# A diffusion layer with product-key experts: 28 multiply-adds handed to ScalarE and GpSimd, 13 steps moved ahead, gate chunks on GpSimd's queue

## The chip, the cores and the metric

The kernel runs on one core of one Trainium2 chip. The metric is device time in microseconds (us) of one execution. The core has TensorE (PE in the profile), VectorE (DVE), ScalarE (ACT), GpSimd (POOL), and SyncE (SP), which here only issues transfers.

## The reference, cut to what matters

One layer is computed for 128 context tokens (tile 0) and 512 latent tokens (tiles 1 to 4). Its second half is a retrieval over 16384 single-neuron experts:

```
def _peer(h, w_query, sub_keys, expert_u, expert_v):          # per block of 128 tokens
    q = (xb @ w_query).reshape(t, 8, 2, 128)
    s = einsum('thik,hink->thin', q, sub_keys)                # 8 heads, two halves of 128 keys
    v_half, i_half = top_k(s, 16)
    top_v, top_pos = top_k(v_half[0] + v_half[1] (16 x 16), 16)
    idx = i_half[0] * 128 + i_half[1] at top_pos              # 8 x 16 = 128 picks per token
    g = softmax(top_v)
    act = gelu(einsum('thkd,td->thk', expert_u[idx], xb))
    return einsum('thk,thkd->td', g * act, expert_v[idx])
```

Each token has 128 picks. For each pick the kernel needs a dot product with a row of `expert_u` (1024 numbers) and a multiply-add of a row of `expert_v`.

## The kernel before, in words

The program of each engine is written out by hand, in order, with semaphores between the engines. Up to about 1340 us of the profiled execution it does the token-mixing half of the layer; the change does not touch that. The retrieval is done in two ways.

**Gathered tiles.** Context tile 0 and latent tiles 1 and 2 (the code calls the latter "apart") have their rows gathered: for pick k GpSimd issues an indirect DMA of 128 rows of 4 KB (512 KB) of `peer_u` (`u_row`) and one of `peer_v` (`v_row`). VectorE does the dot (`u_dot`, line 1999) and the multiply-add into a sum of 128 x 1024 (`v_add`, line 2021; semaphore `vc_used` counts them). The v side runs 20 picks behind the u side for the context (`LEAD`) and 40 behind for the apart tiles (`APART_LEAD`). A "context step" j is `u_dot(j)` and `v_add(j - 20)`, 148 of them; an "apart step" j is `u_dot(128 + j)` and `v_add(128 + j - 40)`, 296 of them. The rows land in ten buffers of 4 KB a partition; the u rows and the v rows use four each, for some stretches eight, and GpSimd waits in `row_free` until the row that stood in the buffer has been used. GpSimd's loop interleaves the u row of step j and the v row of step j in one queue.

**Whole tiles.** Tiles 3 and 4 are done densely. PE multiplies them with blocks of all of `peer_u` (128 blocks of 512 KB, `s_block`, line 1112; ScalarE takes each with a Gelu, line 1531, `take_s`), the result is multiplied with a gate matrix, and PE multiplies that with the blocks of `peer_v` (`v_block`, line 1143). The gate matrix is built from one-hot rows in 64 units (the "build": VectorE lines 2168 and 2178, ScalarE lines 1566 and 1557, PE line 1130). Half of the gates stays in SBUF, half goes to HBM (`gates_far`), comes back in 16 chunks of 512 KB made of 512-byte pieces (`load_gates`, two buffers, on SyncE's queue between the expert blocks) and is multiplied in by GpSimd (`gate_block`, line 1702, 64 of them).

**The order of the last half.** Stretches, by what VectorE and PE do:

1. Heads (from 1410 us). PE makes queries in 16 halves (line 1070) and scores, ScalarE copies them out (`take_queries`, lines 1484 to 1493). VectorE finds for each head the 16 best of tiles 3 and 4 (two calls of `top`), then runs `CTX_BESIDE[h]` context steps, for some heads a `top` of an apart tile, and `APART_BESIDE[h]` apart steps; at head 6 it finishes tile 0 (`result(0, ...)`), which needs ScalarE's `tile_norm(0)`.
2. First half of the blocks. PE runs 64 `s_block`s. ScalarE's program pins other work to them by number n: `tile_norm(0)` behind n = 20, the Exp of the whole tiles' weights (`ew_done`, line 1542) behind n = 44, and the Exp and Gelu of the first apart items (`gates`, lines 1329 and 1330) behind n = 54, 58 and 62. VectorE meanwhile does `SOFTMAX_AT` = 8 apart steps, `weigh_whole` (line 2157, needs `ew_done`), and the rest of `APART_EARLY` steps. From apart step 40 on a v row is added, and ahead of it `weights(8)` (line 2009) needs the `gates` behind n = 54. `APART_TOP_AT` says behind which step a `top` of an apart tile stands.
3. Build, with single apart steps between the units (`APART_BUILD`).
4. Between: 64 pairs of `v_block` and `s_block` on PE, and 104 apart steps spread beside them (`START_BETWEEN`). `gate_block(n)` stands in GpSimd's queue behind step `START_BETWEEN + (20 + n) * 104 // 64`.
5. Last: 64 `v_block`s of the second half, all remaining apart steps, the last results.

```
CTX_BESIDE = (5, 5, 5, 5, 4, 4, 0, 0)
APART_TOP_AT = {16 * n - 9: n for n in range(3, 2 * PH)}
APART_EARLY = 34
APART_BUILD = [int(u % 6 == 1) for u in range(UNITS)]
START_1 = sum(APART_BESIDE) + APART_EARLY
```

Of the kernel before, what the change touches and what calls it, by code (L numbers as in the profile page):

```python
# [5 lines left out]

# [65 lines left out]
def q_end(who, name):  # L72
    return Q[who, name] + len(TILES[who])
# [78 lines left out]
def row_slot(kind, k):  # L152

    j = k - PICKS
    if kind == "u":
        if j < 0:
# [4 lines left out]


ROW_ORDER = ([row for j in range(PICKS + LEAD) for row in [("u", j)] * (j < PICKS) + [("v", j - LEAD)] * (j >= LEAD)]
             + [row for j in range(2 * PICKS + APART_LEAD)
# [132 lines left out]
def layer_kernel(nc, a, outs):  # L297

    y_out, st_out = outs
    with ExitStack() as ctx:  # L300
# [130 lines left out]
        rowbuf = [at(kb, D) for kb in (166, 170, 174, 186, 92, 96, 190, 194, 110, 114)]  # L431
        pv_c, pv_a = at(135.25, D), [at(16, D), at(178, D)]
        tables_c = [at(125.75 + 0.5 * i, PICKS) for i in range(3)]
        tables_a = [at(kb, 2 * PICKS) for kb in (198, 199, 108)]
# [36 lines left out]
        def s(name):  # L471
            if name not in S:
# [9 lines left out]
                 "keys_in keys_l_in fq_full fq_out fs_full fs_out sc_full sc_free topk_done topw_done ge_done w_done u_used "  # L482
                 "vc_used pv_done out_ready out_done ew_done gw_done tw_full tw_out ieq_done ihot_done jhot_done "
                 "g_full g_done gs_staged gm_done s_full s_out av_done dve act waited")
# [28 lines left out]
        def _(sp):  # L513
# [142 lines left out]

            far = gates_far.rearrange("g p (i t) -> p g i t", i=HALF)

            def load_gates(c):

                if c >= 2:
                    sp.wait_ge(s("gm_done"), CHUNK * (c - 1))
                sp.dma_start(gates_in[c % 2], far[:, :, CHUNK * c:CHUNK * c + CHUNK, :]).then_inc(gates_sem[c % 2], 16)

            for n in range(HALF):
# [4 lines left out]
            for q in range(2):  # L670
                sp.wait_ge(staged_out[q], 8 * GROUPS)
            chunks = iter(range(HALF // CHUNK))
            for n in range(HALF, len(BLOCKS)):
                load_block(n)
                passed = (n - HALF) // 2 if n < 3 * HALF else HALF + (n - 3 * HALF) // 2
                if n == HALF + NSLOT:
                    load_gates(next(chunks))
                    load_gates(next(chunks))
                if n % 2 and passed >= MULT_LAG + 7 and (passed - MULT_LAG - 7) % CHUNK == 0:
                    c = next(chunks, None)  # L680
                    if c is not None:
                        load_gates(c)
            for c in chunks:
                load_gates(c)
            sp.wait_ge(s("out_done"), 16 * NT)
# [480 lines left out]
        def _(act):  # L1166
# [339 lines left out]

            late = list(range(GATES_DONE, PH))
            take_queries(0, (0,))
            take_queries(1, (0,))
# [10 lines left out]
            take_scores(PH - 1)  # L1520

            def take_s(n, i):
# [10 lines left out]
            for n, i in enumerate(FIRST_ORDER):  # L1533
                take_s(n, i)
                if n == 20:
                    act.wait_ge(s("vc_used"), PICKS)
# [44 lines left out]
            for n, item in enumerate(APART_GATES.get(("last",), [])):  # L1581
                gates(item)
                if n == 0:
                    act.wait_ge(s("vc_used"), 2 * PICKS)
# [17 lines left out]
            store(4, 4)  # L1602
            act.wait_ge(s("vc_used"), 3 * PICKS)
            ch.n += 2
# [6 lines left out]
        def _(pool):  # L1611
# [33 lines left out]
            def row_free(kind, k):  # L1645

                before = ROW_BEFORE[ROW_NUMBER[kind, k]]
                if before is not None:
                    kind_before, k_before = ROW_ORDER[before]
                    pool.wait_ge(s("u_used" if kind_before == "u" else "vc_used"), k_before + 1)  # L1650

# [8 lines left out]
            def v_row(k):  # L1660
# [5 lines left out]
                    bass.IndirectOffsetOnAxis(ap=entries(IDX, k), axis=0)).then_inc(row_in[slot], 16)  # L1666

            pool.wait_ge(s("sc_free"), 4)
            for j in range(CSTEPS):
                if j < PICKS:  # L1670
# [24 lines left out]

            rows_of_apart(START_1)
            def gate_block(n):

# [6 lines left out]
            for j in range(START_BETWEEN, ASTEPS):  # L1705
                rows_of_apart(1)
                for n in MULTS_AT.get(j, []):
                    gate_block(n)


        @block.vector
        def _(dve):
# [299 lines left out]
            def v_add(k):  # L2012
# [6 lines left out]
                else:  # L2019
                    dve.wait_ge(s("vc_used"), k)  # L2020
# [140 lines left out]
            def equal(u):  # L2161
# [30 lines left out]
            for h in range(PH):  # L2192
# [84 lines left out]
```

## Time and profile before

| | |
|---|---|
| time, median of 3 runs | 2803.74 us (2794.14 to 2809.4) |
| the profiled execution | 2781.54 us, its span 2779.7 us |
| PE busy | 2354.6 us, 85% of the span |
| DVE busy | 1839.6 us, 66% |
| POOL busy | 1117.4 us, 40% |
| ACT busy | 612.3 us, 22% |
| indirect gathers | 768 of 512 KB, 402.70 MB of 701.59 MB in all |

A row of a timeline gives start, duration, engine, line and operation, output and input, the number of instructions, and in brackets how long the engine sat idle before it and whom it waited for. "DMA share" is the mean busy share of the 16 DMA engines (values a little over 1 are full), GB/s is what they moved. Busy shares over the whole span say little here, since each stretch has its own bound.

### The profile page before, as it was taken

The page shows a single profiled execution, that of the slowest core. Times are in us where ns is not written, and L with a number is a line of the kernel's source. Part 1 is how long each engine was busy: PE and PEld are TensorE (multiplying, and loading weights), DVE is VectorE, ACT ScalarE, POOL GpSimd, SP SyncE. Part 2 cuts the span into 40 slices and gives each one's busy share as a digit, 9 for nine tenths or more (in the row PEclk, how much of TensorE's full clock was granted, in tenths as well). Part 3 has the DMA queues.
Part 4 walks back from the last instruction along what each step waited for, and adds up shares of the span by engine and source line. Part 5 has one row for each costly group of instructions (what it writes and reads, how often), then busy time and mean ns, then how long its engine had stood idle before and what let it go on. Part 6 is the DMA issues. An engine that isn't in the chain of part 4 may idle for free.

```text
span 2779.7 us, 26765 instructions
## 1 busy us (share of the span) xinstructions
PE 2354.6 (85%) x8858; PEld 1476.9 (53%) x8858; DVE 1839.6 (66%) x3451; ACT 612.3 (22%) x1483; POOL 1117.4 (40%) x928
## 2 busy tenths in 40 slices
PE   6998888899999998999979999576899999999500
PEld 1354544544555544578468888465566666444200
DVE  0335767744100569787779997999775677676988
ACT  0113452522211113311222112384000000100010
POOL 0002312221000125777433234525574767666575
PEclk9899999999999999999989999788999999999855
DMA  7601111213284558999765689746998999999998
GB/s 268 222 31 33 51 38 30 68 38 127 74 269 173 177 190 300 380 369 401 270 266 198 234 310 340 295 167 252 406 397 330 390 400 403 386 401 410 373 334 292
DMA packets 251301, 701.59 MB, mean 252 GB/s; under 512 B 20912, under 2 KB 62000, under 8 KB 249904
## 3 DMA queue, kind: packets, MB, share of 16 engines
q0 software_dynamic: 110592, 402.70, 38.6%
q1 hardware_dynamic: 139872, 294.79, 29.4%
q10 hardware_dynamic: 720, 2.62, 0.2%
q8 instruction: 63, 1.03, 0.1%
q14 instruction: 54, 0.44, 0.0%
HBM read 686.93 MB, written 13.11 MB: 252 GB/s over the span
## 4 chain that ended last, share of the span: by engine, by line
PE 53%; DVE 16%; DMA 14%; POOL 8%; issue 5%; ACT 3%; DVEq 0%; SPq 0%; ACTq 0%; POOLq 0%
PE bank L1112 14%; PE bank L896 11%; PE bank L1143 8%; POOL arena L1664 4%; DMA arena<-in_peer_v,arena 4%; PE bank L1070 4%; PE bank L750 4%; DMA arena<-in_peer_v 3%; POOL arena L1656 3%; DVE arena L2168 3%; DVE arena L2021 2%; PE bank L791 2%; DVE arena L1807 2%; DMA arena<-in_w_ada 2%; PE bank L709 2%
## 5 line engine op out<-in xcount | busy, mean ns | idle before, releaser
L1656 POOL DMA_INDIRECT arena<-in_peer_u,arena x384 | 477.1, 1242 | 789.1 <-DVE arena L1999 429.4
L2021 DVE SCALAR_TENSOR_TENSOR arena<-arena 128x1024 f32<-128x1024 f32 x381 | 495.0, 1299 | 118.7 <-DMA arena<-in_peer_v,arena 112.6
L1999 DVE CUSTOM_DVE_ANT_0 arena<-arena 128x1024 f32<-128x1024 f32 x384 | 475.6, 1244 | 147.5 <-DMA arena<-in_peer_u,arena 147.1
L1664 POOL DMA_INDIRECT arena<-in_peer_v,arena x384 | 461.4, 1202 | 226.5 <-DVE arena L2021 115.9
L896 PE MATMUL bank<-arena 128*128 128x512 f32 (+1 forms) x1472 | 510.0, 508 | 16.5 <-DMA arena<-in_w_in 6.5
L1143 PE MATMUL bank<-arena 128*128 128x512 f32 x1024 | 453.2, 595 | 22.4 <-DMA arena<-in_peer_v 22.4
L1112 PE MATMUL bank<-arena 128*128 128x256 f32 x2048 | 455.1, 380 | 14.6 <-DMA arena<-in_peer_ut 13.9
L1112 PEld LDWEIGHTS bank<-arena 128*128 128x128 f32 x2048 | 390.4, 191 | 95.8 <-issue 30.1
L896 PEld LDWEIGHTS bank<-arena 128*128 128x128 f32 x1472 | 283.2, 194 | 239.1 <-issue 198.6
L1143 PEld LDWEIGHTS bank<-arena 128*128 128x128 f32 x1024 | 194.4, 191 | 243.3 <-issue 224.0
L750 PE MATMUL bank<-arena 128*128 128x512 f32 x384 | 182.0, 621 | 7.9 <-ACT arena L1207 6.5
L1531 ACT ACTIVATE arena<-bank 128x256 f32<-128x256 f32 x128 | 49.0, 383 | 606.3 <-PE bank L1112 606.2
L1629 POOL TENSOR_TENSOR arena<-arena 128x512 f32<-128x512 f32 x40 | 45.1, 1127 | 268.6 <-ACT arena L1255 268.6
L1620 POOL TENSOR_TENSOR arena<-arena 128x512 f32<-128x512 f32 x32 | 42.5, 1362 | 257.2 <-DVE arena L1818 257.2
L1130 PE MATMUL bank<-arena 128*128 128x128 f32 x512 | 86.1, 335 | 62.7 <-ACT arena L1566 62.6
L750 PEld LDWEIGHTS bank<-arena 128*128 128x128 f32 x384 | 72.9, 198 | 87.1 <-issue 83.3
L1130 PEld LDWEIGHTS bank<-arena 128*128 128x128 f32 x512 | 78.8, 242 | 70.2 <-ACT arena L1566 41.2
L1070 PE MATMUL bank<-arena 128*128 128x256 f32 x512 | 112.9, 381 | 0.7 <-ACT arena L1458 0.7
L709 PE MATMUL bank<-arena,cond_sb 128*2 128x512 f32 x192 | 84.8, 600 | 27.2 <-DMA arena<-in_w_ada 27.2
L1807 DVE SCALAR_TENSOR_TENSOR arena<-arena,convw_sb 128x644 f32<-128x644 f32 x96 | 99.5, 1037 | 11.4 <-DVE arena L1807 1.1
L1070 PEld LDWEIGHTS bank<-arena 128*128 128x128 f32 x512 | 97.3, 191 | 13.9 <-ACT arena L1458 1.0
L1255 ACT ACTIVATE arena<-bank,arena 128x128 f32<-128x128 f32 x320 | 86.6, 396 | 50.9 <-PE bank L841 50.7
(237 smaller groups left out, 2389.4 us busy)
## 6 DMA issues: line engine op xcount, KB each, us to landing
arena<-in_peer_ut SPq DMA_DIRECT2D x128, 512.0 KB, 6.9
arena<-in_peer_v SPq DMA_DIRECT2D x128, 512.0 KB, 8.5
arena<-in_w_in SPq DMA_DIRECT2D x22, 2048.0 KB, 9.0
arena<-in_w_ada SPq DMA_DIRECT2D x12, 2048.0 KB, 8.0
arena<-in_w_ssd_out SPq DMA_DIRECT2D x8, 2048.0 KB, 16.2
arena<-in_w_query SPq DMA_DIRECT2D x8, 2048.0 KB, 9.0
arena<-in_w_fourier SPq DMA_DIRECT2D x4, 2048.0 KB, 7.8
arena<-in_w_out SPq DMA_DIRECT2D x4, 2048.0 KB, 13.4
```

The source lines that it names most:

```text
L709: last = mm(bank[slot][0:2, :], cond[:, k, :], w[:, k, :], start=(k == 0), stop=(k == KT - 1))
L750: mm(bank[2][:, :], w[:, k, c0:c0 + P], hT[:, k, P:TOK], start=(k == 0), stop=(k == KT - 1), skip_group_check=True)
L896: last = mm(bank[q % 5][:, 0:cols], rows_of(k), w[:, k, :], start=(k == 0), stop=(k == k_tiles - 1))
L1070: last = mm(bank[n % 4][:, 0:2 * P], w[:, k, c0:c0 + P], h2Tp[1 - pair][:, k, :], start=(k == 0), stop=(k == KT - 1))
L1112: last = mm(bank[4 + n % 2][:, 0:2 * P], ut[:, k, :], h2Tp[1][:, k, :], start=(k == 0), stop=(k == KT - 1))
L1130: last = mm(bank[GATE_BANKS[u % 6]][:, P * t:P * t + P], hot_j[u % HOTS][:, t, :], hot_i[u % HOTS][:, t, :], start=True, stop=True)
L1143: last = mm(bank[2 * t + half][:, :], Aw[:, i % HALF, t * P:t * P + P], v[:, 512 * half:512 * half + 512], start=(i == 0), stop=(i == NKEY ...
L1656: nc.gpsimd.indirect_dma_start(rowbuf[slot], None, a["peer_u"], bass.IndirectOffsetOnAxis(ap=entries(IDX, k), axis=0)).then_inc(row_in[slo ...
L1664: nc.gpsimd.indirect_dma_start(rowbuf[slot], None, a["peer_v"], bass.IndirectOffsetOnAxis(ap=entries(IDX, k), axis=0)).then_inc(row_in[slo ...
L1807: last = STT(o, cin[:, i % 2, k:k + 644], w(k), o, ALU.mult, ALU.add)
L1999: V.tensor_tensor_reduce(out=rowbuf[slot], in0=rowbuf[slot], in1=h2c if item < PH else h2a[:, item // PH - 1, :], scale=1.0, scalar=0.0, o ...
L2021: STT(pv, rowbuf[slot], w, pv, ALU.mult, ALU.add).then_inc(s("vc_used"), 1)
```

## The change

The last 28 picks of the context (k = 100 to 127, `BY_POOL`) are no longer multiplied and added by VectorE. ScalarE scales the gathered row in place with its weight (`scale_rows`), two rows behind each of the halves 2 to 15 of the queries; GpSimd adds the scaled rows into a sum `pv_g` of its own (`add_scaled`, 27 adds of 128 x 1024), and VectorE adds that sum to its own once, at head 5. The `u_dot`s stay on VectorE. A buffer of those v rows comes free by GpSimd's add (`vg_used`), so the gather of row k now waits for the adds of row k - 4 and stands behind `u_row` in the same queue.

The context steps beside the heads become (8, 8, 8, 8, 0, 0, 0, 0), most of them empty. The apart steps ahead of the build go from 24 + 34 = 58 to 24 + 43 = 67, those in the build from 11 to 15; 104 stay between, and 110 are left for the last stretch in place of 123. The `top`s stand 5 steps earlier (steps 34, 50, 66, ...), so three of them and not two are ahead of the build. The second half's gate chunks are issued by GpSimd: two at step 12 of the between stretch, each further one right behind the `gate_block` that frees its buffer. The first one-hot rows wait for block 60 and not 64, and ScalarE's last context gates stand behind half 5 and not 8.

```diff
-CTX_BESIDE = (5, 5, 5, 5, 4, 4, 0, 0)
+CTX_BESIDE = (8, 8, 8, 8, 0, 0, 0, 0)
+BY_POOL = range(100, PICKS)
-APART_TOP_AT = {16 * n - 9: n for n in range(3, 2 * PH)}
-APART_EARLY = 34
+APART_TOP_AT = {16 * n - 14: n for n in range(3, 2 * PH)}
+APART_EARLY = 43
-APART_BUILD = [int(u % 6 == 1) for u in range(UNITS)]
+APART_BUILD = [int(u % 4 == 2 and u < 60) for u in range(UNITS)]
...
@@ sync
             for n in range(HALF, len(BLOCKS)):
                 load_block(n)
-                passed = (n - HALF) // 2 if n < 3 * HALF else HALF + (n - 3 * HALF) // 2
-                if n == HALF + NSLOT:
-                    load_gates(next(chunks))
-                    load_gates(next(chunks))
-                if n % 2 and passed >= MULT_LAG + 7 and (passed - MULT_LAG - 7) % CHUNK == 0:
...
@@ scalar
+            def scale_rows(n, item):
+                for k in itertools.islice(to_scale, n):
+                    slot = row_slot("v", k)
+                    act.wait_ge(s("w_done"), k // TOPK + 1)
+                    act.wait_ge(row_in[slot], 16 * ROW_TURN[ROW_NUMBER["v", k]])
+                    A(rowbuf[slot], rowbuf[slot], ACT.Copy, scale=entries(WTAB, k)).then_inc(s("scaled"), 1)
...
                 if half % 2 == 0:
                     take_scores(half // 2 - 1)
-                if half == 8:
+                if half == 5:
                     for item in late:
                         gates(item)
+                scale_rows(2, 6 if half < 8 else 7)
...
@@ gpsimd
+            def add_scaled(k):
+                pool.wait_ge(s("scaled"), k - BY_POOL[0] + 1)
+                if k == BY_POOL[0]:
+                    return
+                scaled = rowbuf[row_slot("v", k)]
+                if k == BY_POOL[1]:
+                    TT(pv_g, rowbuf[row_slot("v", k - 1)], scaled, ALU.add).then_inc(s("vg_used"), 1)
+                else:
+                    pool.wait_ge(s("vg_used"), v_count(k))
+                    TT(pv_g, pv_g, scaled, ALU.add).then_inc(s("vg_used"), 1)
...
+                if j - LEAD == BY_POOL[4]:
+                    add_scaled(next(to_add))
+                    add_scaled(next(to_add))
+                elif j - LEAD > BY_POOL[5]:
+                    add_scaled(next(to_add))
                 if j >= LEAD:
                     v_row(j - LEAD)
+            for k in to_add:
+                add_scaled(k)
...
+                if j == START_BETWEEN + 12:
+                    for q in range(2):
+                        pool.wait_ge(staged_out[q], 8 * GROUPS)
+                    load_gates(0)
+                    load_gates(1)
                 for n in MULTS_AT.get(j, []):
                     gate_block(n)
+                    if n % CHUNK == CHUNK - 1 and n // CHUNK + 2 < HALF // CHUNK:
+                        load_gates(n // CHUNK + 2)
...
@@ vector
-                if j >= LEAD:
+                if j >= LEAD and j - LEAD not in BY_POOL:
                     v_add(j - LEAD)
...
-                        dve.wait_ge(s("s_full"), HALF)
+                        dve.wait_ge(s("s_full"), max(n + 1 for n in range(HALF) if B_SLOT[n] >= 4))
...
+                if h == 5:
+                    dve.wait_ge(s("vc_used"), BY_POOL[0])
+                    dve.wait_ge(s("vg_used"), len(BY_POOL) - 1)
+                    TT(pv_c, pv_c, pv_g, ALU.add).then_inc(s("vc_used"), 1)
```

## Rows read from the trace of the kernel before

**Rows 1.** Windows: us; PE, PEld, DVE, ACT, POOL busy (instructions); PEclk; DMA share; GB/s.
```profile
1420.00:1540.00 120.00, 119.23 (x613) 106.54 (x614) 99.75 (x317) 24.40 (x59) 30.44 (x24) 1.00 0.51 173
...
1787.00:1912.00 125.00, 86.09 (x512) 78.81 (x512) 125.00 (x227) 99.56 (x320) 33.30 (x24) 0.82 0.46 157
...
2383.00:2500.00 117.00, 111.42 (x258) 48.23 (x256) 81.72 (x121) 10.46 (x16) 78.93 (x68) 1.00 1.03 400
2500.00:2780.00 280.00, 110.13 (x256) 48.56 (x256) 229.83 (x339) 17.18 (x35) 179.41 (x156) 0.71 0.93 352
```

**Rows 2.** Timeline of PE, the end of the first 64 blocks.
```profile
1719.26 41.60 PE L1112 MATMUL bank<-arena 128*128 128x256 f32 x192
```

**Rows 3.** Timeline of DVE, heads to build.
```profile
1439.61 0.43 DVE L1951 MAX8 arena<-arena 128x8 f32<-128x256 f32 x1
...
1448.64 0.43 DVE L1951 MAX8 arena<-arena 128x8 f32<-128x256 f32 x1
...
1453.71 1.22 DVE L1999 CUSTOM_DVE_ANT_0 arena<-arena 128x1024 f32<-128x1024 f32 x1
...
1456.06 1.22 DVE L1999 CUSTOM_DVE_ANT_0 arena<-arena 128x1024 f32<-128x1024 f32 x1
...
1636.60 0.15 DVE L2138 RECIPROCAL arena<-arena 128x1 f32<-128x1 f32 x1
...
1701.91 0.41 DVE L2157 TENSOR_REDUCE arena<-arena 128x16 f32<-128x256 f32 x1
...
1733.37 0.17 DVE L2009 RECIPROCAL arena<-arena 128x1 f32<-128x1 f32 x1 [2.22 <-ACT arena L1330]
...
1787.25 4.96 DVE L2168 TENSOR_TENSOR arena<-shape_consts,arena 128x512 f32<-128x512 f32 x8
```

**Rows 4.** Timeline of ACT in the same stretch.
```profile
1451.52 0.66 ACT L1493 ACTIVATE arena<-bank 128x256 f32<-128x256 f32 x2 [0.30 <-PE bank L1082]
...
1538.21 0.66 ACT L1493 ACTIVATE arena<-bank 128x256 f32<-128x256 f32 x2 [0.30 <-PE bank L1082]
...
1614.48 0.29 ACT L1499 ACTIVATE arena<-arena,eps 128x1 f32<-128x1 f32 x1
...
1696.33 0.42 ACT L1542 ACTIVATE arena<-arena 128x256 f32<-128x256 f32 x1
...
1733.13 0.22 ACT L1330 ACTIVATE arena<-arena 128x16 f32<-128x16 f32 x1
```

**Rows 5.** Timeline of POOL: the gather of u row 124, context.
```profile
1455.21 1.74 POOL L1656 DMA_INDIRECT arena<-in_peer_u,arena  x1 [30.37 <-DVE arena L1999]
```

**Rows 6.** Single lines: count, ns minimum/median/maximum, first and last start, form.
```profile
L1702 POOL TENSOR_TENSOR arena<-arena x64: 723/745/1794, 2031.4 to 2514.0; 128x256 f32<-128x256 f32 x64
...
L1629 POOL TENSOR_TENSOR arena<-arena x40: 1038/1039/1462, 260.1 to 655.8; 128x512 f32<-128x512 f32 x40
...
L1498 ACT ACTIVATE arena<-arena x3: 1040/1048/1056, 1612.0 to 2772.4; 128x1024 f32<-128x1024 f32 x3
```

**Rows 7.** Waits: who waited for whom, us, times, longest.
```profile
POOL arena L1702 <- DMA arena<-gates_far: 80.6, 11, 24.0
```

**Rows 8.** DMA issues: engine, count, KB each, median us to landing.
```profile
arena<-gates_far SPq DMA_DIRECT2D x16, 512.0 KB, 17.7
arena<-in_peer_u,arena POOLq DMA_INDIRECT x384, 8.5
```

**Rows 9.** Windows of line 2021 alone (x is v rows added): DVE busy, PEclk, DMA share, GB/s.
```profile
1921.00:2021.00 100.00, 29.58 (x23) 0.92 1.03 405
2021.00:2121.00 100.00, 27.37 (x20) 1.00 0.93 355
2121.00:2221.00 100.00, 26.76 (x20) 1.00 1.01 387
...
2612.00:2655.00 43.00, 17.61 (x14) 0.56 0.87 330
2655.00:2704.00 49.00, 21.02 (x17) 0.50 0.97 355
```

More of the change, by code:

```diff
@@ L5 @@
 from contextlib import ExitStack, contextmanager
+import itertools
 import numpy as np
@@ L160, in row_slot, with v_count @@
     return V_ROWS[k % 4] if late < 0 else (V_ROWS + LATE_ROWS)[late % 8]
+def v_count(k):
+    if k in BY_POOL:
+        return max(0, k - BY_POOL[0] - 1)
+    return k if k < PICKS else k - len(BY_POOL) + 1
 ROW_ORDER = ([row for j in range(PICKS + LEAD) for row in [("u", j)] * (j < PICKS) + [("v", j - LEAD)] * (j >= LEAD)]
@@ L432, in layer_kernel @@
         pv_c, pv_a = at(135.25, D), [at(16, D), at(178, D)]
+        pv_g = at(16, D)
         tables_c = [at(125.75 + 0.5 * i, PICKS) for i in range(3)]
@@ L482, in layer_kernel @@
                  "keys_in keys_l_in fq_full fq_out fs_full fs_out sc_full sc_free topk_done topw_done ge_done w_done u_used "
-                 "vc_used pv_done out_ready out_done ew_done gw_done tw_full tw_out ieq_done ihot_done jhot_done "
+                 "vc_used vg_used scaled pv_done out_ready out_done ew_done gw_done tw_full tw_out ieq_done ihot_done jhot_done "
                  "g_full g_done gs_staged gm_done s_full s_out av_done dve act waited")
@@ L655, in load_block @@
                 sp.dma_start(blocks[B_SLOT[n]], src).then_inc(b_in[B_SLOT[n]], 16)
[L657 to L663, printed above, removed]
             for n in range(HALF):
@@ L671, in _ @@
                 sp.wait_ge(staged_out[q], 8 * GROUPS)
-            chunks = iter(range(HALF // CHUNK))
             for n in range(HALF, len(BLOCKS)):
                 load_block(n)
-                passed = (n - HALF) // 2 if n < 3 * HALF else HALF + (n - 3 * HALF) // 2
-                if n == HALF + NSLOT:
-                    load_gates(next(chunks))
-                    load_gates(next(chunks))
-                if n % 2 and passed >= MULT_LAG + 7 and (passed - MULT_LAG - 7) % CHUNK == 0:
[L680 to L684, printed above, removed]
             sp.wait_ge(s("out_done"), 16 * NT)
@@ L1507, in _ @@
             late = list(range(GATES_DONE, PH))
+            to_scale = iter(BY_POOL)
+            def scale_rows(n, item):
+                for k in itertools.islice(to_scale, n):
+                    assert k // TOPK <= item, k
+                    slot = row_slot("v", k)
+                    act.wait_ge(s("w_done"), k // TOPK + 1)
+                    act.wait_ge(row_in[slot], 16 * ROW_TURN[ROW_NUMBER["v", k]])
+                    A(rowbuf[slot], rowbuf[slot], ACT.Copy, scale=entries(WTAB, k)).then_inc(s("scaled"), 1)
             take_queries(0, (0,))
@@ L1516, in _ @@
                     take_scores(half // 2 - 1)
-                if half == 8:
+                if half == 5:
                     for item in late:
                         gates(item)
+                scale_rows(2, 6 if half < 8 else 7)
             take_scores(PH - 1)
+            assert next(to_scale, None) is None
             def take_s(n, i):
@@ L1535, in _ @@
                 if n == 20:
-                    act.wait_ge(s("vc_used"), PICKS)
+                    act.wait_ge(s("vc_used"), v_count(PICKS))
                     tile_norm(0, pv_c, h2c)
@@ L1583, in _ @@
                 if n == 0:
-                    act.wait_ge(s("vc_used"), 2 * PICKS)
+                    act.wait_ge(s("vc_used"), v_count(2 * PICKS))
                     act.wait_ge(s("topk_done"), NORM_TOPS)
@@ L1602, in _ @@
             store(4, 4)
-            act.wait_ge(s("vc_used"), 3 * PICKS)
+            act.wait_ge(s("vc_used"), v_count(3 * PICKS))
             ch.n += 2
@@ L1649, in row_free @@
                     kind_before, k_before = ROW_ORDER[before]
-                    pool.wait_ge(s("u_used" if kind_before == "u" else "vc_used"), k_before + 1)
+                    if kind_before == "u":
+                        pool.wait_ge(s("u_used"), k_before + 1)
+                    else:
+                        pool.wait_ge(s("vg_used" if k_before in BY_POOL else "vc_used"), v_count(k_before) + 1)
             def u_row(k):
@@ L1666, in v_row @@
                     bass.IndirectOffsetOnAxis(ap=entries(IDX, k), axis=0)).then_inc(row_in[slot], 16)
+            def add_scaled(k):
[5 more added lines that the diff above has]
+                    TT(pv_g, rowbuf[row_slot("v", k - 1)], scaled, ALU.add).then_inc(s("vg_used"), 1)
+                else:
+                    pool.wait_ge(s("vg_used"), v_count(k))
+                    TT(pv_g, pv_g, scaled, ALU.add).then_inc(s("vg_used"), 1)
             pool.wait_ge(s("sc_free"), 4)
+            to_add = iter(BY_POOL)
             for j in range(CSTEPS):
@@ L1696, in _, with load_gates @@
             rows_of_apart(START_1)
+            far = gates_far.rearrange("g p (i t) -> p g i t", i=HALF)
+            def load_gates(c):
+                if c >= 2:
+                    pool.wait_ge(s("gm_done"), CHUNK * (c - 1))
+                nc.gpsimd.dma_start(gates_in[c % 2], far[:, :, CHUNK * c:CHUNK * c + CHUNK, :]).then_inc(gates_sem[c % 2], 16)
             def gate_block(n):
```

2 lines of the change are left out of this document (1 added, 1 removed).

## The prediction

> **What bounds the kernel now.** I read first the windows, one per stretch, since the busy shares of the page mix stretches with different limits. In the heads PE is busy all the time (119 of 120 us) and DMA only half [rows 1]. In the build VectorE has no idle time (125.00 of 125.00) and nothing else is full [rows 1]. Behind it, to 2500 us, the DMA engines are full (share 1.03, about 400 GB/s), and even at the end they stand at 0.93 [rows 1]: there an apart step costs what its two gathers of 0.524 MB cost beside PE's blocks. I read next the timelines of DVE, ACT and PE side by side to see what sets the start of the build. PE has its 64 blocks done at 1719.26 + 41.60 = 1760.9 [rows 2]; VectorE begins the build at 1787.25 [rows 3]. So VectorE is late by 26 us, and what happens on it sets the path. The reader is to see one more thing: at 1733.37 VectorE's `weights(8)` waited 2.22 us for ScalarE's Gelu behind block 54, which ended at 1733.35 [rows 3, 4]. So VectorE came there at 1731.1, and this point is given by PE's blocks, not by VectorE. Last I read who waits for the gate chunks (80.6 us of GpSimd [rows 7]) and the rate of v rows at the end [rows 9].
>
> All sums are made against the profiled execution (2781.5 us, span 2779.7), which is 22 us under the median of the runs shown (2803.7); I carry the difference over to the median. What a measurement of this kernel can tell from no change is about 0.5%, 14 us.
>
> **Part 1: 28 multiply-adds leave VectorE.** A context step with both parts takes 1456.06 - 1453.71 = 2.35 us, of which the dot is some 1.15 (its 1.22 overlaps a little with what follows), so the v part is 1.20 [rows 3]. 28 of them are 33.6 us; one add of the two sums comes back, 1.2. VectorE would reach `result(0)`, before at 1636.6 [rows 3], some 32 us earlier, less what it loses on late rows (below, some 10 us: the dots 124 to 127 now stand in GpSimd's queue behind adds). But what comes next on VectorE waits for ScalarE's work that is pinned to PE's blocks: `tile_norm(0)` was done at 1614.8, the Exp for `weigh_whole` at 1696.75, and the Gelu for step 40 at 1733.35 [rows 4]. From `weigh_whole` (1701.9) to step 40 (1731.1 without the wait) are 29 us before [rows 3]; the top that now stands at step 34 was at 39, so it is in this stretch either way. An early VectorE starts that stretch at 1696.75 at best and has it done by 1726, ahead of 1733.35. So the 33.6 us freed go into waits, and step 40 begins where PE's blocks say. Value of part 1 by itself: 0. If no pin held, it would be 22 to 32 us; that end is rival D.
>
> **Part 2: what the new work does to PE.** ScalarE's scaling of a row is like line 1498, 1.05 us [rows 6]; 28 of them are 29 us on an engine that is busy 24 of 120 us there [rows 1], so its time is hidden. Its waits are not. ScalarE's program is in order: behind `scale_rows` stand the copies of the next queries and scores, and for them PE waits (four banks). Rows 100 to 103 are there early. Row 104's gather stands behind the gather of u row 124, which waits for VectorE's dot 120 until 1455.2 [rows 5], and behind the first add. With 1.74 for that issue [rows 5], the add and the next issue it leaves at about 1460 to 1461, lands up to 8.5 us later [rows 8] (sooner, since DMA is half idle) and is scaled at about 1469. ScalarE stood there at 1452.2 before [rows 4]. From row 104 on each v row needs one issue (about 1.24 with the gap) and one add on GpSimd.
>
> The add of 128 x 1024 is not in the trace. From below: two of 128 x 512 with a repeated operand are 2.08, with one start-up less perhaps 1.7; from above: four of 128 x 256 are 2.98 [rows 6]. I take 2.4, nearer to the 256-wide row, which like it has two full operands. That is 3.64 a row, 3.8 with some waits. 23 rows more from 1469: 1556; then the last scores are copied (1.5 us), and the first block starts at about 1556 to 1558, where it started at 1538.9 (the copy of 1538.21 + 0.66 [rows 4]). PE's own pace, 86.7 us from the copy of scores 1 to that of scores 7 for 11 halves, is 7.9 a half or 3.9 a row [rows 4], so with a cheap add PE only loses the one stall, about 7 us; with an add of 2.98 it is 4.4 a row and 31 us. Delay of all blocks, and so of the pins: 17 us, between 7 and 31. Nothing of it can be a gain.
>
> The Trainium skill, GPSIMD Engine Reference, section "Elementwise — side-by-side cycle accounting", gives 4497 ns for an add of 2048 floats; half of it is 2.25 us, an estimate from that page, and the sum would be about 4 us lower.
>
> **Part 3: 9 steps and one top more ahead of the build.** All of them lie behind the pin of step 40. Before: from 1733.37 to 1787.25 are 53.9 us for 18 steps (40 to 57) and one top. A top is 1448.64 - 1439.61 = 9.03 us [rows 3], so a step is 2.49. After: 27 steps (40 to 66) and two tops (50, 66), 67.2 + 18.1 = 85.3, that is +31.4. The path to the build is then 1733.35 + 17 + 85.3 = 1835.7: PE is done with its blocks at 1761 + 17 and waits. The wait for block 60 in place of 64 costs and brings nothing, since VectorE comes later than both.
>
> **Part 4: 4 steps more in the build.** VectorE is full there, so each costs its 2.35: +9.4; one item of ScalarE's Exp and Gelu now falls into the build, +1. Sum to the start of "between": 31.4 + 17 + 10.4 = +59.
>
> **Part 5: 13 steps less at the end.** PE's last block ends at about 2612 (110 us of PE behind 2500 [rows 1], with few gaps). In the windows 2612 to 2704 are 14 + 17 = 31 steps with both rows in 92 us, and one top (step 231) [rows 9]; without it 2.68 a step. Behind them come the same v rows alone as before. With 13 steps less 18 are left there, and the last top (226) has then been done beside PE: 48 us in place of 92, -44. If the top were not hidden, -35.
>
> **Part 6: the gate chunks.** GpSimd stood 80.6 us for chunks, up to 24 at a time [rows 7], with a chunk landing 17.7 us after its issue on SP's queue [rows 8]. The stalls do not count as such, as DMA is full nearly always; what counts is where it wasn't: 355 and 387 GB/s in two windows of 100 us beside 405 [rows 9], 6.8 MB or 6.5 steps of 1.05 MB. Each done earlier saves 2.68 at the end: -17. From below: 0 (DMA is full by other means). From above -25. Price of the issue on GpSimd, not in the trace: one like a gather's, about 1 us, or, by pieces (1024 against the gather's 128), up to 8 times that, 8 us. 16 of them are 16 to 128 us. A step in that stretch takes 100 / 22 = 4.5 us [rows 9] and GpSimd needs two issues (2.6), 0.6 of a gate multiply of about 1, and 1/6.5 of a chunk's issue: 3.4 to 4.4 us, just within. I take some 4 us each, hidden by DMA being the slower.
>
> **Sum.** +31.4 + 17 + 10.4 - 44 - 17 = -2 us. Predicted: 2779 us for the profiled execution, 2801 for the median. No change that can be told.
>
> **Rivals.**
> A, slower: GpSimd is the place where it fails. A chunk's issue at the upper bound and an add at 2.98: 31 us of delay and no gain by the chunks give +31.4 + 31 + 10.4 - 44 = +29 (2833); with the delay as taken and only the chunks' gain lost it is +15 (2819). It decides from a chunk issue of about 8 us, where GpSimd's 4.4 a step meets the 4.5 of DMA. For it: nearly everything of the change is put into GpSimd's one queue. Against: GpSimd has idle time in every stretch [rows 1]. 0.25.
> B, slower: VectorE and GpSimd hold each other up. The 128 x 256 multiply takes 0.745 at the median and 1.794 at most [rows 6], so something makes it wait by 1.05 for a VectorE operation. If that befalls each of the 27 adds, a row is 4.85, the delay 23 x 1.05 = 24 more, in all +22 (2826). Against: VectorE's operations in the heads are mostly short ones with one input. 0.07. The Trainium skill, SBUF — State Buffer, section "SBUF: two separate sides", calls the port pair that VectorE operations with two SBUF inputs and GpSimd share an exclusive lock; the trace agrees with 0.745 and 1.794.
> C, faster: the delay is only PE's one stall, 7 us, and the chunks bring 25: -2 - 10 - 8 = -20 (2784). For it: two bounds that are each possible. 0.20.
> D, faster: the pins don't hold VectorE, since it comes to them late for another reason, and the 32 us freed are kept: build start about where it was, -2 - 48 = -50 (2754). Against: 1733.35 is in the trace. 0.06.
> Forecast (within 14 us of before): 0.42.
>
> **Numbers.** Slower by over 0.5%: A and B without the part of A that stays under 14 us, 0.30. Faster: C and D and a little of the forecast's edge, 0.28. Same: 0.42. The range goes from C's better half to A: 2771 to 2834; the forecast's own is 2790 to 2817.
>
> **What would show it.** Right: ScalarE waiting for gathers (`in_peer_v`) at its new scaling line, and PE idle among the queries; the first block at about 1556; VectorE idle before `result(0)`, before `weigh_whole` and, by some 10 us or more, before `weights(8)`; the build starting at about 1835 and lasting 135; no waits of line 1702 for `gates_far`; 18 or fewer steps with both rows behind PE's last block. Wrong: a build that starts at or before 1800 (pins or delay misjudged); chunk issues of over 8 us on GpSimd; a DMA share under 1 in the between stretch; a v-row pace at the end other than 2.7.

## The result, and the profile after

The changed kernel takes 2803.56 us (median of 22 runs, 2793.67 to 2813.82) where the kernel before takes 2797.01 in 22 runs beside it: ratio 1.0026, 95% interval [1.0014, 1.0037]. That is 7 us slower, under the 0.5% that I called a change, but on the other side of zero than my sum of -2.

The first profiled execution of before (2781.54) was a short one, below all 22 others; a second took 2790.93 and is used below. Those of after took 2810.69 and 2808.77, 5 to 7 us above its median of 2803.56. So two profiles differ by 11 to 13 us more than the medians do, and what one term is worth is read from timed experiments. One unit serves throughout: (ratio - 1) x 2795 us. Most intervals below reach 4 to 6 us to either side (7 for i2), so a difference of two kernels is known to about 8 us.

After, the windows that answer to [rows 1]:

```profile
1423.00:1543.00 120.00, 111.92 (x552) 98.72 (x553) 90.22 (x253) 44.11 (x74) 79.30 (x49) 0.97 0.55 184
1845.00:1970.00 125.00, 77.65 (x472) 69.36 (x472) 124.89 (x224) 95.25 (x301) 39.98 (x28) 0.87 0.50 165
2400.00:2520.00 120.00, 116.27 (x308) 58.76 (x307) 83.55 (x147) 12.40 (x21) 77.68 (x66) 0.99 0.98 378
```

In the heads PE now loses 8 of 120 us and GpSimd is busy for 79 instead of 30. In the build VectorE is still the full one. The timeline of PE says when each stretch begins:

```profile
1472.60 3.78 PE L1074 MATMUL bank<-arena 128*128 128x128 f32 x16 [4.35 <-ACT arena L1476]
...
1560.29 9.90 PE L1104 MATMUL bank<-arena 128*128 128x256 f32 x38 [7.45 <-ACT arena L1485]
...
1742.31 41.61 PE L1104 MATMUL bank<-arena 128*128 128x256 f32 x192
...
1847.38 8.44 PE L1122 MATMUL bank<-arena 128*128 128x128 f32 x48 [63.46 <-ACT arena L1571]
...
1991.86 3.75 PE L1135 MATMUL bank<-arena 128*128 128x512 f32 x4 [12.04 <-DMA arena<-in_peer_v]
```

PE is idle for ScalarE among the queries, the first block comes at 1560.3, PE has its 64 blocks done at 1783.9 [rows 2: 1760.9], and then waits 63 us for the build. VectorE, in answer to [rows 3] (the combining add, `result(0)`, `weigh_whole`, `weights(8)`, the build):

```profile
1619.02 1.22 DVE L2244 TENSOR_TENSOR arena<-arena 128x1024 f32<-128x1024 f32 x1
...
1647.39 0.16 DVE L2181 RECIPROCAL arena<-arena 128x1 f32<-128x1 f32 x1
...
1719.83 0.42 DVE L2200 TENSOR_REDUCE arena<-arena 128x16 f32<-128x256 f32 x1 [7.99 <-ACT arena L1547]
...
1756.43 0.16 DVE L2052 RECIPROCAL arena<-arena 128x1 f32<-128x1 f32 x1 [9.22 <-ACT arena L1322]
...
1845.22 1.28 DVE L2211 TENSOR_TENSOR arena<-shape_consts,arena 128x512 f32<-128x512 f32 x2
```

With 28 multiply-adds less on it, VectorE comes to `result(0)` at 1647.4, 11 us later than before [rows 3: 1636.6], not 22 to 32 earlier; 2.9 of the 11 us are a later start of the heads (their first MAX8 on VectorE is at 1438.6 instead of 1435.7). The new operations themselves, line by line (GpSimd's adds, the chunk issues, ScalarE's scaling):

```profile
L1686 POOL TENSOR_TENSOR arena<-arena x26: 2342/2362/2438, 1468.0 to 1560.5; 128x1024 f32<-128x1024 f32 x26
...
L1731 POOL DMA_DIRECT2D arena<-gates_far x16: 944/969/969, 2018.2 to 2531.9; - x16
...
L1509 ACT ACTIVATE arena<-arena x28: 1133/1151/1178, 1439.4 to 1558.1; 128x1024 f32<-128x1024 f32 x28
its engine sat idle before it (us, times) until:
  DMA arena<-in_peer_v,arena: 46.1, 16
```

The last two rows are ScalarE's waits for gathered rows, 46.1 us, with the copies that PE's next queries need queued behind them. The waits of `gate_block` for chunks are gone, as forecast (before: 80.6 us [rows 7]), but behind PE's last block 24 steps with both rows are left (27 in c2), where the prediction had 18 or fewer.

### The profile page after: what moved, and what is told of

It reads as the page before. It is cut to its first block, busy times and chain, and to the rows that moved or that the text cites. A ratio compares the mean times of both kernels' runs of the same rounds, so it can differ in the third digit from the quotient of the medians.

```text
span 2808.5 us, 26823 instructions
## 1 busy us (share of the span) xinstructions
PE 2359.2 (84%) x8858; PEld 1476.8 (53%) x8858; DVE 1839.9 (66%) x3424; ACT 641.3 (23%) x1511; POOL 1218.7 (43%) x971
## 4 chain that ended last, share of the span: by engine, by line
PE 32%; DVE 21%; POOL 17%; DMA 16%; issue 10%; ACT 3%; DVEq 0%; SPq 0%; ACTq 0%; POOLq 0%
PE bank L888 11%; POOL arena L1672 8%; DMA arena<-in_peer_v,arena 7%; PE bank L1104 7%; POOL arena L1664 6%; DMA arena<-in_peer_u,arena 4%; PE bank L742 4%; DVE arena L2064 3%; DVE arena L2211 2%; DVE arena L2042 2%; PE bank L783 2%; DVE arena L1850 2%; DMA arena<-in_w_ada 2%; PE bank L701 2%; POOL arena L1738 1%
## 5 line engine op out<-in xcount | busy, mean ns | idle before, releaser
L1664 POOL DMA_INDIRECT arena<-in_peer_u,arena x384 | 488.4, 1272 | 863.0 <-DVE arena L2042 505.0
L2064 DVE SCALAR_TENSOR_TENSOR arena<-arena 128x1024 f32<-128x1024 f32 x353 | 460.6, 1305 | 123.7 <-DMA arena<-in_peer_v,arena 115.7
```

Source lines behind the costliest of these rows:

```text
L1664: nc.gpsimd.indirect_dma_start(rowbuf[slot], None, a["peer_u"], bass.IndirectOffsetOnAxis(ap=entries(IDX, k), axis=0)).then_inc(row_in[slo ...
```

## The experiments

**The two kernels again.** No edit.

> The kernel before once more, unchanged, for a second profile: the first one (2781.54) lay 15 us below the median of the unprofiled runs, while the changed kernel's (2810.69) lay 7 us above its own. If that first profile was an exceptionally fast execution, the new one comes out at 2790 to 2800 and the stretches that I compared (from the first read of a context block to the end, 858.5 us) were about 10 us too short for before; if profiled executions simply differ from unprofiled ones by a fixed amount, it repeats at 2780 to 2785 and the changed kernel's repeats at 2808 to 2812. Ratio 1.000 either way.

> The changed kernel once more, unchanged, for a second profile. Ratio 1.002 to 1.003 as before. If the profiles scatter, it lies anywhere between 2796 and 2812; the build should again start about 1845 and the first read of a context block come about 1992, since those follow from the order of work and not from the transfers.

Ratios 0.9993 [0.9977, 1.0009] and 1.0028 [1.0010, 1.0045]. The profiles took 2790.93 and 2808.77 us, both in the ranges named. PE reads the first block of `peer_v` (`v_block`; the expectations call it the first context block) at 1925.1 and 1988.1.

**Which edit costs what.** The chunks put back or moved alone, the order of the steps alone, the adds alone:

```
a1: changed kernel,  load_gates(c) on SyncE between the blocks, as before
b1: kernel before,   load_gates(c) on GpSimd, as changed
s1: kernel before,   APART_TOP_AT 16*n - 14, APART_EARLY 43, APART_BUILD u % 4 == 2 and u < 60
d1: changed kernel,  the three numbers of s1 as before, load_gates on SyncE
k1: s1 + b1
```

> The changed kernel with the gate chunks fetched by SyncE again, all else as changed. Theory 1 (the prediction's step 6: chunks between the blocks on SyncE stall the products and keep the transfers from running full): 14 to 20 us slower than the changed kernel, 2818 to 2824, ratio to the kernel before about 1.009. Theory 2 (the transfers are full either way, 391 against 394 GB/s in the two profiles, so that a stall of the products only moves bytes from one moment to the next): within 4 us of the changed kernel, ratio 1.001 to 1.004. Theory 3 (what GpSimd spends on issuing, 16 times 0.95 us, and what it waits, costs more than it saves): 5 to 15 us faster than the changed kernel.

> The kernel before with one edit of the change alone: GpSimd fetches the gate chunks. Theory 1 (step 6 is worth 17 us): 2776 to 2784, ratio 0.993 to 0.996. Theory 2 (transfers full either way): within 4 us of the kernel before, ratio 0.999 to 1.001. Theory 3 (GpSimd pays more than it saves): ratio 1.002 to 1.005.

> The kernel before with the order of the steps alone: 43 steps before and 15 in the build, later top positions; no sum on GpSimd, chunks on SyncE. Theory 1 (steps pay for themselves; the block delay is what the change loses): the first context block about 41 us later (31 ahead of the build, 10 in it), the time from there to the end about 47 us shorter, as it is between the unchanged kernel's second profile (864) and that of the changed kernel with its chunks on SyncE (817): about 2790, ratio 0.997 to 0.999. Rival (steps cost as much as they save or more, and the block delay is nothing): 2800 or more, ratio 1.001 to 1.004.

> The changed kernel with the steps in their old order and the chunks on SyncE: only the 28 multiply-adds by ScalarE and GpSimd are left of the change. Theory 1: blocks 18 us later and nothing gained on VectorE, since what ScalarE does behind fixed blocks holds it: 2810 to 2816, ratio 1.005 to 1.008; the build starts 18 us later than in the kernel before. Rival (the adds gain VectorE 36 us, part of which is kept): the build starts earlier than in the kernel before, ratio 0.99 to 1.00.

> The kernel before with two of the three edits: the new order of the steps and the gate chunks by GpSimd; context's multiply-adds stay on VectorE. It is the fourth corner of a square with the kernel before (2796), the chunks alone (2778) and the steps alone (2788). Theory 1 (the two add up): about 2770, ratio 0.990 to 0.992. Theory 2 (they don't, since with the steps moved the stretch from the first context block to the last dot product already runs at 391 GB/s, so that chunks without a stall leave more steps behind TensorE's last block instead): 2784 to 2790, ratio 0.996 to 0.998, and that stretch 730 to 738 us long.

| kernel | adds | steps | chunks on GpSimd | ratio, 95% | us |
|---|---|---|---|---|---|
| b1 | | | x | 0.9937 [0.9916, 0.9959] | -18 |
| s1 | | x | | 0.9974 [0.9956, 0.9993] | -7 |
| k1 | | x | x | 0.9970 [0.9953, 0.9987] | -8 |
| d1 | x | | | 1.0080 [1.0057, 1.0103] | +22 |
| a1 | x | x | | 1.0032 [1.0010, 1.0053] | +9 |
| c2 | x | x | x | 1.0028 [1.0010, 1.0045] | +8 |

The adds are a loss in each pair: +22 (d1), +16 (s1 to a1), +16 (k1 to c2). The steps are worth 7 us while the chunks are on SyncE (13 beside the adds, d1 to a1) and cost 9 when they are on GpSimd (b1 to k1). The chunks are worth 18 us in the old order and 1 in the new one (s1 to k1, a1 to c2); the 17 us between these two are beyond the noise, while the 1 can't be told from 0. The adds with the chunks on GpSimd in the old order weren't run. For b1 theory 1 held, for a1 theory 2: no single theory named both. For s1 and d1 theory 1 held (d1 at the upper end of its range; its build starts 20 us later than in c1, both counted from the first MAX8 of the heads), for k1 theory 2.

Where these 18 us go is seen in two windows for each kernel: from the first `v_block` to the end of PE's last block, and from there to the last dot product. First the second profile of before, then b1:

```profile
1925.00:2620.00 695.00, 669.19 (x2048) 391.49 (x2048) 477.95 (x797) 62.42 (x124) 441.30 (x371) 0.98 1.00 388
2620.00:2711.00 91.00, 0.00 (x0) 0.00 (x0) 79.65 (x125) 3.09 (x5) 64.60 (x56) 0.52 0.90 325
```

```profile
1927.00:2593.00 666.00, 662.83 (x2048) 389.57 (x2048) 467.83 (x781) 59.32 (x119) 449.35 (x376) 1.00 1.02 397
2593.00:2696.00 103.00, 0.23 (x1) 0.00 (x0) 92.81 (x141) 6.18 (x10) 76.01 (x67) 0.52 0.94 341
```

And with the steps moved, s1 and then k1:

```profile
1970.00:2656.00 686.00, 667.27 (x2048) 390.86 (x2048) 478.13 (x795) 59.32 (x119) 435.31 (x372) 0.99 1.01 391
2656.00:2701.00 45.00, 0.00 (x0) 0.00 (x0) 42.44 (x53) 3.09 (x5) 34.11 (x33) 0.56 1.01 396
```

```profile
1970.00:2640.00 670.00, 665.92 (x2048) 390.98 (x2048) 470.24 (x784) 59.38 (x119) 458.40 (x378) 0.99 1.01 393
2640.00:2702.00 62.00, 0.46 (x2) 0.00 (x0) 53.82 (x67) 3.09 (x5) 48.09 (x43) 0.54 0.97 363
```

The reader is to see that PE's own work is 663 to 669 us in all four. With chunks on SyncE PE has 19 to 26 us of stalls on top, without them 3 to 4, and the first window ends sooner. But DMA moves at most some 400 GB/s over these windows, so a shorter first window holds fewer steps: by their dots 155 in before's, 150 in b1's, 155 in s1's, 151 in k1's. What was not done is left behind PE's last block, 29, 34, 17 and 22 steps (a few records are missing). Both windows together: 786 us for before and 769 for b1, at 381 and 389 GB/s for the same 299 MB; 731 and 732 for s1 and k1, both at 391 GB/s for 286 MB. So the chunks pay where the rate was low, and s1 had lifted it already, above all behind PE's last block (396 in place of 325 GB/s). One reason is seen there: in before and b1 a `top` falls behind PE's last block, and in the 20 us from about its start DMA moves 244 and 268 GB/s; in s1 and k1 none does. GpSimd's waits for chunks say nothing of the time: 83.0 us in s1, none in k1. The profile of s1 (2781.18) is 6 us below its median, so its 731 us may be some us short.

**Scaling later.** The same 28 rows, but scaled where they have come; `half == 5` back to 8. In g1 and j2 also some of ScalarE's pinned work moved.

```
f1: changed kernel, rows scaled behind halves 2,3,7,9,...,15 (2 or 1 each) and blocks 0..10 (1 each)
g1: f1 + tile_norm(0) behind block 14 (20), Exp behind 38 (44), first gates behind 46, 54, 62 (54, 58, 62)
j2: f1 + only the last two of these
```

> The changed kernel with the same 28 rows scaled, but two or one at a time later in ScalarE's order (the last ones behind block 10), at places where the row and its weight have come, and with the eighth item's gates taken behind half 8 as in the kernel before. Theory 1 (TensorE's 18 us of delay come from ScalarE's waits for rows and for the dot products ahead of the copies that free the banks): the first block comes 14 to 18 us earlier than in the changed kernel, the build too, 2785 to 2790, ratio 0.996 to 0.998. Rival (the delay of the blocks doesn't matter, as GpSimd's sum sets the end of the context and VectorE's work is behind it): ratio 1.001 to 1.004, as changed.

> The same, and the three pieces of ScalarE's work that VectorE waits for behind fixed blocks come earlier: the square of the context behind block 14 and not 20, the exponential behind block 38 and not 44, the next gates behind block 46 and not 54. Theory 1 (these places hold VectorE, so what GpSimd took over is waited away): another 10 to 30 us, 2756 to 2780, ratio 0.986 to 0.993, and VectorE's three waits (8.0 and 9.2 us and what stands ahead of them) shrink. Rival (the work behind those places has no room to come earlier: the context is only done by then): within 4 us of the version without them.

> The version with the rows scaled later (2788), whole sums, with the exponential behind block 38 and the next gates behind block 46, the square of the context left behind block 20: 12 us were lost when that one was moved to block 14, as TensorE then stood 18.5 us. If these two places hold VectorE (3.0 us of waits are left in that version): 2784 to 2787. If nothing of VectorE waits for them: 2786 to 2790.

f1: 0.9967 [0.9951, 0.9983], 17 us faster than the changed kernel (c2); its first block starts at 1539.1, 17 us earlier than c2's 1556.4, and ScalarE waits for no row at its scaling line any more. Theory 1 held: the block delay of the adds is ScalarE's waiting (the gates back behind half 8 are in the same edit and weren't tried alone). Beside k1, the same kernel with the multiply-adds on VectorE (-8), f1 is at -9: without the delay the handing over is worth nothing that can be told. g1: 1.0023 [1.0006, 1.0039], which contradicts my theory; j2: 0.9974 [0.9958, 0.9990], nothing beside f1. The timeline of PE in g1 shows why:

```profile
1615.95 24.33 PE L1105 MATMUL bank<-arena 128*128 128x256 f32 x104 [18.54 <-ACT arena L1536]
```

ScalarE stood at the context's square until the sum was there (1611) and did not take PE's banks. Behind block 14 is too early for a context that is done no sooner. But it should have been done sooner: VectorE had 28 multiply-adds less.

**What GpSimd's sum does to VectorE.** Groups of VectorE's instructions by form from 1440 to 1620: the kernel before (second profile), then the changed one.

```profile
L2021 DVE SCALAR_TENSOR_TENSOR arena<-arena 128x1024 f32<-128x1024 f32 x28 | 36.0, 1284 | 2.9 <-DMA arena<-in_peer_v,arena 1.4
L1999 DVE CUSTOM_DVE_ANT_0 arena<-arena 128x1024 f32<-128x1024 f32 x16 | 19.1, 1224 | 0.0
...
L1983 DVE TENSOR_TENSOR arena<-arena 128x512 bf16<-128x512 bf16 x14 | 5.9, 425 | 0.5
L1976 DVE TENSOR_SCALAR arena<-arena 128x16 f32<-128x16 f32 x13 | 3.0, 234 | 0.5
L1988 DVE COPY arena<-arena 128x16 f32<-128x16 f32 x24 | 3.0, 171 | 0.4
```

```profile
L2026 DVE TENSOR_TENSOR arena<-arena 128x512 bf16<-128x512 bf16 x14 | 17.1, 1222 | 0.5
L2042 DVE CUSTOM_DVE_ANT_0 arena<-arena 128x1024 f32<-128x1024 f32 x8 | 14.4, 1832 | 10.5 <-DMA arena<-in_peer_u,arena 10.5
L2031 DVE COPY arena<-arena 128x16 f32<-128x16 f32 x24 | 12.7, 575 | 0.4
L2023 DVE TENSOR_TENSOR arena<-iota,arena 128x512 bf16<-128x512 bf16 x14 | 9.7, 692 | 0.5
...
L2019 DVE TENSOR_SCALAR arena<-arena 128x16 f32<-128x16 f32 x14 | 8.5, 608 | 0.5
...
L2014 DVE TENSOR_TENSOR arena<-arena 128x256 f32<-128x256 f32 x14 | 5.8, 416 | 0.0
L2022 DVE CAST arena<-arena 128x32 bf16<-128x32 uint32 x14 | 5.0, 359 | 0.5
```

The same 14 `top`s of the same forms: the bf16 product costs 425 ns and then 1222, the copy 171 and 575, the small subtraction (TENSOR_SCALAR) 234 and 608, the cast 182 and 359, the dot 1224 and 1832. That is 11.2 + 9.7 + 5.2 + 2.5 + 4.9 = 33.5 us more, and 10.5 us of waiting for u rows, against 36.0 us taken away. (The dots are 8 in place of 16 because the steps of head 5 come behind 1620 in the changed kernel.) Such a copy beside GpSimd's add (2.68 us for two copies of 0.17 each), first on VectorE, then GpSimd's add:

```profile
1520.19 2.68 DVE L2031 COPY arena<-arena 128x16 f32<-128x16 f32 x2
```

```profile
1520.39 2.37 POOL L1686 TENSOR_TENSOR arena<-arena 128x1024 f32<-128x1024 f32 x1
```

The copies end 0.1 us behind the add. The Trainium skill, SBUF — State Buffer, section "SBUF: two separate sides", has GpSimd and a VectorE operation with two SBUF inputs, or in a mode that uses both port pairs, as an fp32 copy from SBUF to SBUF does, exclude each other for the whole of an instruction; the copies and the bf16 products (2.65 to 2.67 us beside a whole add) agree, and it is VectorE that waits: GpSimd's adds stay within 2342 to 2438 ns. Two forms with two inputs did not lengthen, the comparison L2023 (692 ns in both kernels) and the fp32 sum L2014 (419 and 416). In the timeline from 1480 to 1565 they fall between two adds or reach into one by less than 0.3 us, so they are no test.

To see what this costs, 26 of the 27 adds were cut to 8 of 1024 columns, so the context's sum leaves the rest of those rows out:

```
i1: f1, TT(pv_g[:, 0:8], pv_g[:, 0:8], scaled[:, 0:8], ALU.add)
i2: i1, tile_norm(0) behind block 18, Exp behind 38, first gates behind 46, 54, 62
```

> The version with the rows scaled later, but 26 of GpSimd's 27 sums are cut to 8 of 1024 columns, so that the context is wrong in the rest: it shows what these sums cost VectorE. Theory P (ports: while GpSimd adds, VectorE's short two-operand and copy forms last two to three times as long, 34 us in all between 1440 and 1620 of the changed kernel, and that eats the 36 us that were taken off VectorE): those forms are back at 425, 171, 234 and 181 ns, the context is done earlier or more dot products are done by then, and the build starts 10 to 30 us earlier than with the whole sums; 2760 to 2778, ratio 0.987 to 0.994. Theory Q (my prediction's: places in ScalarE's order hold VectorE anyway): the forms are short, but VectorE then waits for ScalarE by as much; 2784 to 2790.

> The same cut sums (context wrong in all but 8 columns), and ScalarE's square of the context behind block 18 instead of 20, the exponential behind block 38 instead of 44, the next gates behind block 46 instead of 54. Theory P alone: no different from the cut sums without it, within 4 us. Theory Q, or both one after the other: 8 to 20 us faster than that, 2745 to 2770, because VectorE's freed time then has somewhere to go.

In i1 these forms are back (the dot isn't: 1361 ns, in f1 1371), and VectorE waits for ScalarE instead (groups by form, then the timeline of DVE, of i1):

```profile
L2027 DVE TENSOR_TENSOR arena<-arena 128x512 bf16<-128x512 bf16 x15 | 6.4, 426 | 0.5
L2020 DVE TENSOR_SCALAR arena<-arena 128x16 f32<-128x16 f32 x16 | 3.7, 234 | 0.6
L2032 DVE COPY arena<-arena 128x16 f32<-128x16 f32 x26 | 3.5, 182 | 0.5
```

```profile
1586.64 1.22 DVE L2245 TENSOR_TENSOR arena<-arena 128x1024 f32<-128x1024 f32 x1
...
1701.25 0.42 DVE L2201 TENSOR_REDUCE arena<-arena 128x16 f32<-128x256 f32 x1 [14.50 <-ACT arena L1548]
...
1737.85 0.16 DVE L2053 RECIPROCAL arena<-arena 128x1 f32<-128x1 f32 x1 [9.32 <-ACT arena L1323]
```

The context is summed at 1586.6 instead of 1610.8 (f1), 28 us earlier when counted from the first MAX8 of the heads, and 23.8 us are then waited away at the two pins (3.0 in f1): ratio 0.9957 [0.9939, 0.9975], 3 us from f1 and within both intervals. That is theory Q. i2, with the pins moved too, takes 0.9929 [0.9904, 0.9955], 11 us from f1 and from k1, 13 from j2 and 8 from i1. This fits two obstacles in series, each of which eats the saving alone: removing only two pins (j2) or only the long adds (i1) gives nothing, both give 11 us of the 36. It is not fully isolated: i2 rests on four runs, its 8 us from i1 are just at the noise, and it also moves `tile_norm(0)` by two blocks, which j2 doesn't. Much of the rest is waited for gathered u rows (35 us of VectorE's waits between the heads and the build in i2, 10 in before; all its idle time there is 64 and 39 us).

**How many steps ahead.** From b1, the fastest so far. The `top`s had to move with the steps, as none may fall into the build.

```
m1: b1, APART_EARLY 26, APART_TOP_AT 16*n - 15
m2: b1, APART_BUILD u % 4 == 2 and u < 60 (15), APART_TOP_AT 16*n - 7
m3: b1, both, APART_TOP_AT 16*n - 15
b2: b1 again
```

> The kernel before with the gate chunks by GpSimd (2778), and 8 steps fewer ahead of the build (26 for 34; tops six positions earlier, so that none falls into the build). If a step ahead costs what the timeline shows (2.5 us and no top here, 20 us in all) and one behind is worth 2.6 to 3.0 us (a step's two rows are 1.05 MB, at 400 GB/s 2.6 us): 2777 to 2783, no difference that can be told. If a step left over costs 4.6 us, as the pair before and steps alone gave with the chunks on SyncE: 2790 or more.

> The same with 34 steps ahead, as before, but 15 in the build instead of 11. Four steps at 2.4 us make the build 10 us longer, and four fewer behind it are worth 10 to 12 us at 2.6 to 3.0 us: 2775 to 2779. If the two edits' loss against the chunks alone (2785 against 2778) lies in the build: 2783 or more.

> Both: 26 ahead and 15 in the build. By the same prices 2775 to 2782.

> The kernel before with the gate chunks by GpSimd once more, as the measure for the three beside it: 2775 to 2780, ratio 0.992 to 0.995, as before. If the first measurement was a lucky one, it comes out at 2782 to 2786, with the version that has both edits.

Ratios: m1 0.9963 [0.9948, 0.9978], m2 1.0006 [0.9989, 1.0022], m3 0.9969 [0.9954, 0.9984], b2 0.9932 [0.9911, 0.9952]. b1 holds (-18 and -19 us). All times count from the first MAX8 of the heads: in m1 the first `v_block` comes 20 us earlier than in b2, 8 steps at 2.5 us as expected; from there to the last dot are 797 us instead of 771, so 8 steps more cost 26 us there, 3.2 each and not 2.6 to 3.0. Its 2784.68 us lie between the two ranges named. m2 missed by 20 us: its build starts 8 us later with the same 34 steps ahead, because the `top` of step 39 became that of step 41 and so stands behind the pin of step 40, where it is no longer covered; four steps in the build are another 8.4 us; and nothing is got back (776 us to the last dot, with 4 steps less). m3 is -13 us at the first `v_block`, as the prices say, and 793 us behind it.

## Why the prediction was wrong

The failed step is part 6, the gate chunks: "Each done earlier saves 2.68 at the end: -17", added to part 5's -44 in the sum. Measured in the kernel it was written for (a1 to c2) the term is -1, known to about 8 us. Without it my sum is +15 for a kernel that measures +9 (a1). Alone on the kernel before the same term measures -18 (b1), so its size was right for the wrong kernel: I read the two low windows from before [rows 9] and took parts 5 and 6 to be independent. They draw on the same thing, DMA below 400 GB/s between the first `v_block` and the last dot. With 13 steps less the rate there goes from 381 to 391 GB/s without the chunks' edit, and with that edit it stays at 391. So what the runs show in place of -17 is: the stalls of PE go (19 us in s1, 4 in k1), the rate does not rise, and the steps that the shorter first window doesn't hold are done behind PE's last block.

Why the rate stays at 391 is not settled. One place is seen where k1 loses: in the 20 us from the start of the `top` some 425 us into the first window DMA falls to 321 GB/s in b1, 271 in k1 and 276 in c2. Yet in s1 and a1, with the same places of the `top`s and the chunks on SyncE, it is 404 GB/s there. So this fall goes with the chunks on GpSimd's queue and not with the places of the `top`s alone. It was not isolated.

Point by point. **Part 1**, no gain by itself: right in size (f1 beside k1) and right in that the pins would hold (i1), but the size was in part luck. I had VectorE coming to `result(0)` some 22 to 32 us early and waiting; it came 11 us late, and the freed time was gone before a pin could take it. What I had as rival B at 0.07 was real and reversed: not GpSimd's add but VectorE's short operations are held up. "VectorE's operations in the heads are mostly short ones with one input" was no protection.

**Part 2:** the add took 2.36 us (taken 2.4), row 104 was scaled at 1467.8 (1469), the blocks came 18.5 us late once the 2.9 us of a later start of the heads are taken off (17). d1 prices it at +22, s1 to a1 at +16, and f1 takes it back (-17).

**Parts 3 to 5:** 88.8 us from step 40 to the build (85.3); the build starts at 1845.2 and not 1835.7, and of these 9.5 us 2.9 lie ahead of the heads, 1.5 in the delay, 1.6 between first block and pin, 3.5 here. The build lasts 12.1 us longer (10.4). At the end it is 37 us less from the first `v_block` to the last dot where the chunks are moved (b1 to k1) and 55 where they aren't (before to s1), on both sides of the 44 taken. The three together: -2.2 forecast, -7 measured (s1). This is the smaller miss, and it hid some of the larger one: the whole kernel came out 10 us from the sum, with part 6 off by 16.

Of the rivals, A had a true part: the chunks' gain is lost, but not by GpSimd's issues (0.97 us each, the lower bound), and the 15 us it gave for that were 8.

Of the change's edits the chunks alone pay most: b1 beats both kernels, 2777.62 us (median of 7 runs), 18 us faster than before and 25 faster than the changed kernel.

## What to carry to other kernels

When two edits both fill the same resource, price the second one on the kernel that the first leaves: here 18 us of gain were 1. Before a heavy two-operand stream goes to GpSimd, list VectorE's short operations beside it: here they lasted 33.5 us longer. And when work is freed on one engine, look for the next fixed place in another engine's order that it waits for, since two obstacles in series can hide each other from single experiments.

## What the runs showed of the hardware

- VectorE's product of bf16 128 x 512 lasts 425 ns alone and 1222 on average while GpSimd adds 128 x 1024 fp32 (2.36 us each, with a gather's issue of 0.95 us between two adds); single ones reach 2.67 us, the length of an add and 0.3 more. MAX8 and FIND_INDEX8 of 128 x 128 keep their 0.29 and 0.28 us.
- Four other orders of the steps lie 7 to 21 us above b1 and b2, which are one kernel (k1, m1, m2, m3), and single executions of one kernel scatter by up to 27 us (a1: 2792.26 to 2819.62); only timed rounds tell them apart.
- A 512 KB chunk in 512-byte pieces costs GpSimd 0.97 us to issue, about as a gather does (0.94 at the least, 0.98 to 1.00 at the median in after). On SyncE's queue the 16 chunks are 16640 packets, on GpSimd's 2304: before had 110592 packets in q0 and 139872 in q1; the queues of after (packets, MB, share of 16 engines):

```profile
q0 software_dynamic: 112896, 411.09, 39.5%
q1 hardware_dynamic: 123232, 286.40, 28.2%
```
